# Expert stage of a fp32 transformer kernel: four consecutive rows of the down matrix per partition, its loads split by partitions

## The reference, cut to what matters

```python
def moe_swiglu(h, w_router, w_gate, w_up, w_down):
    logits = jnp.einsum('bsd,de->bse', h, w_router).astype(jnp.float32)
    top_v, top_i = lax.top_k(logits, TOP_K)          # 2 of 8 experts
    wts = jax.nn.softmax(top_v, axis=-1)
    gates = jnp.sum(jax.nn.one_hot(top_i, N_EXPERTS, dtype=jnp.float32) * wts[..., None], axis=-2)
    ...
        a = jnp.einsum('sd,edf->sef', hb, w_gate)    # w_gate, w_up: 8 x 1024 x 3584
        u = jnp.einsum('sd,edf->sef', hb, w_up)
        act = jax.nn.silu(a) * u * gb[:, :, None]
        return jnp.einsum('sef,efd->sd', act, w_down)  # w_down: 8 x 3584 x 1024
```

## Time and profile before

| | |
|---|---|
| median of 3 runs | 2482.04 us |
| lowest, highest run | 2480.72, 2488.93 us |
| span of the profiled execution | 2474.2 us |
| part of it in the stage's 56 steps | about 728 to 1708 us |

### The profile page before, as it was taken

The page is one execution under the profiler, slowest core; times in us unless marked ns, Lnnn a source line. Parts: engine busy times, 40 slices in busy tenths (PEclk is TensorE's granted clock), DMA queues, the critical chain, the costliest instruction groups (busy, mean ns, idle before and its releaser), DMA issues. The chain is left out here.

```text
span 2474.2 us, 29768 instructions
## 1 busy us (share of the span) xinstructions
PE 2244.1 (91%) x11037; PEld 1861.1 (75%) x11037; DVE 1815.4 (73%) x1813; ACT 1323.8 (54%) x1336; POOL 49.8 (2%) x130
## 2 busy tenths in 40 slices
PE   3867899797889999999999999996979998887998
PEld 3755788685668888888888888885967888766886
DVE  6987767677779988888888888886745545565444
ACT  2432434354347777777777777775444435344433
POOL 2000000000000000000000000000000000000000
PEclk9978999898899999999999999998989999988999
DMA  8852478744149999999999999997424555322553
GB/s 301 284 202 81 170 278 316 255 158 128 60 154 373 363 349 360 353 359 347 360 352 362 348 360 354 359 364 250 154 85 150 190 192 172 126 74 77 191 173 124
DMA packets 300760, 600.45 MB, mean 243 GB/s; under 512 B 20603, under 2 KB 99174, under 8 KB 300646
## 3 DMA queue, kind: packets, MB, share of 16 engines
q1 hardware_dynamic: 292928, 588.65, 67.2%
q10 hardware_dynamic: 7718, 10.19, 1.2%
HBM read 595.62 MB, written 3.15 MB: 242 GB/s over the span
## 5 line engine op out<-in xcount | busy, mean ns | idle before, releaser
L136 PE MATMUL bank<-ring_rounded,hT_rounded 128*128 128x512 f32 (+3 forms) x912 | 361.4, 396 | 17.8 <-DVE ring_rounded L297 5.7
L136 PE MATMUL bank<-ring_rounded,z_rounded 128*128 128x512 f32 x896 | 355.5, 397 | 0.2 <-DVE ats_rounded L3064 0.2
L136 PE MATMUL bank<-ring_rounded,L_rounded 128*128 128x512 f32 x712 | 283.1, 398 | 13.5 <-DVE ats_rounded L863 11.6
L3060 DVE TENSOR_TENSOR ring_rounded<-ring,zT_rounded 128x2048 fp32r<-128x2048 f32 x110 | 251.0, 2289 | 47.6 <-ACT zT_rounded L2972 47.3
L138 PE MATMUL bank<-zT_rounded,L_rounded 128*128 128x512 f32 x704 | 275.5, 391 | 0.0
L137 PE MATMUL bank<-zT_rounded,ats_rounded 128*128 128x512 f32 x704 | 275.4, 391 | 0.0
L3060 DVE TENSOR_TENSOR ring_rounded<-ring,z_rounded 128x2048 fp32r<-128x2048 f32 x111 | 251.5, 2287 | 18.5 <-ACT z_rounded L2972 17.9
L2972 ACT ACTIVATE z_rounded<-ring 128x2048 fp32r<-128x2048 f32 x111 | 210.8, 1917 | 49.0 <-DMA ring<-in_moe_w_up 31.1
L2972 ACT ACTIVATE zT_rounded<-ring 128x2048 fp32r<-128x2048 f32 x110 | 210.5, 1914 | 22.3 <-DMA ring<-in_moe_w_down 20.8
L136 PEld LDWEIGHTS bank<-ring_rounded,hT_rounded 128*128 128x128 f32 x912 | 175.9, 193 | 53.1 <-issue 14.0
L136 PEld LDWEIGHTS bank<-ring_rounded,z_rounded 128*128 128x128 f32 x896 | 168.3, 188 | 37.6 <-DVE ats_rounded L3064 1.0
(11 more groups left out here) (528 smaller groups left out, 4940.2 us busy)
## 6 DMA issues: line engine op xcount, KB each, us to landing
ring<-in_moe_w_gate SPq DMA_DIRECT2D x224, 512.0 KB, 4.7
ring<-in_moe_w_up SPq DMA_DIRECT2D x224, 512.0 KB, 5.1
ring<-in_moe_w_down SPq DMA_DIRECT2D x224, 512.0 KB, 4.5
ring<-in_ffn_w_gate_up SPq DMA_DIRECT2D x88, 512.0 KB, 5.0
ring<-in_ffn_w_down SPq DMA_DIRECT2D x66, 512.0 KB, 7.9
ring<-in_w_ada SPq DMA_DIRECT2D x48, 512.0 KB, 7.6
ring<-in_w_in SPq DMA_DIRECT2D x32, 512.0 KB, 5.1
xn<-in_w_ada SPq DMA_DIRECT2D x24, 512.0 KB, 9.6
```

Of the source, the lines that this page charges most:

```text
L136: pe.matmul(out, r32(a[0]), r32(b[1]), start=start, stop=False, skip_group_check=True)
L3060: dve.tensor_tensor(r32(w), w, high(c.hi_moe[slot]), ALU.subtract).then_inc(E[kind + '_lo'], 1)
```

## The change

The down matrix is seen as `e (s p a) n -> p (e s) (a n)`: of the 512 rows of a step, partition p holds the four consecutive rows 4p to 4p+3, 16 KB in one stretch of HBM. A slot takes the first or the second 8 KB of it. The two loads of a slot no longer take one row each of all 128 partitions. They take both rows of partitions 0 to 63, and both rows of partitions 64 to 127. Since row 4p+a now stands where row 128a+p stood, DVE writes the activation in the same order: element 4t+a of a token goes to column 128a+t, so that PE's transposes and products stay as they are.

```diff
@@ moe_load
     w, half = c.ring[:, slot, :], s % 2
     if MOE_SLOTS[s] == 'down':
-        w = w.rearrange('p (k n) -> p k n', k=2)
-        for a in range(2):
-            sp.dma_start(w[:, a:a + 1, :], c.moe_down[:, bass.ds(m * ROWS_DOWN + (2 * half + a), 1), :])\
-              .then_inc(sem, 16)
+        for q in range(2):
+            v = slice(q * HD, q * HD + HD)
+            sp.dma_start(w[v, :].unsqueeze(1), c.moe_down[v, bass.ds(m, 1), half * SLOT:half * SLOT + SLOT]).then_inc(sem, 16)
@@ moe_pass_dve, body
-        dve.tensor_tensor(c.moe_fa, c.moe_fs, c.pb[7][:, :], ALU.mult).then_inc(E['act'], 1)
+        dve.tensor_tensor(c.moe_fa.rearrange('p (a t) -> p t a', a=ROWS_DOWN), c.moe_fs.rearrange('p (t a) -> p t a', a=ROWS_DOWN),
+                          c.pb[7][:, :].rearrange('p (t a) -> p t a', a=ROWS_DOWN), ALU.mult).then_inc(E['act'], 1)
@@ build
-        c.moe_down = tensors['moe_w_down'][0].rearrange('e (k p) n -> p (e k) n', p=P)
+        c.moe_down = tensors['moe_w_down'][0].rearrange('e (s p a) n -> p (e s) (a n)', p=P, a=ROWS_DOWN)
```

## The result

The changed kernel takes 2841.88 us (median of 4 runs, 2835.97 to 2847.72), beside 2481.38 us for the kernel before: a ratio of 1.145, 95% interval 1.1423 to 1.1478. It is slower by 360 us. I had forecast 2700 us, slower, with a range up to 2775: the direction was right, and the loss is 1.65 times the 218 us I gave. The medians in this document leave out two runs in a slower state, one of halves_mirrored (2880 us) and one of the kernel before (3835 us).

The account below looks back on a forecast made before the run. PE was taken as the bound at 17.66 us a step; doubled down loads would make DMA the bound at 21.4 us, adding 215 us to a 2474.2 us span, plus 7.8, rounded to 2700 us; range 2476 to 2775.

Parts of the forecast that it names:

- The bound of before: Expert stage: PE sets the pace at 17.66 us a step, DMA second by 0.3 to 1.7 us.
- my two readings of the room: DMA's time for a step's loads: 17.4 us by the 98.3% share, or 16.0 us by the full queue's 393 GB/s.
- The split by partitions: Down loads on one half of the partitions take twice the time, 10.7 us a step instead of 5.3; chance 0.63.
- The sum, 21.4 us a step: Expert stage: 10.7 us for gate and up plus 10.7 for down, above PE's 17.66, so DMA becomes the bound.
- my 215: Expert stage: its last weight matmul ends at 1923 us instead of 1707.8, so the span grows by 215 us.
- Partial sharing as a softening: Down loads: halves overlap as engines drift; 1.8 times gives 2637 us; rival factor 1.3 to 1.8, 2490 to 2635, chance 0.10.
- Longer rows: Down loads: 8 KB rows save about 0.1 us a step, worth nothing while PE sets the pace.
- The product on DVE: L3078, 680 ns before, costs 0.1 us more, covered by 4.1 us; rival that DVE becomes late, up to +38 us, 0.03.
- The clock: Expert stage: PE 83% busy, clock might fall to 0.83, making PE's work 21.3 us; little cost inside the forecast.
- The signs: In the stage: share 100%, 294 GB/s, PE near 83%, SP's waits shrunk, down landings well above gate's, gate packets unchanged.
- The offset: Whole kernel: the median of the runs lies 7.8 us above the span, taking 2689 to 2697 us.
- my own bound by the share reading, 2797: Expert stage: from 17.4 us a step, gate and up 11.6 plus down doubled to 11.6, +315 us.

Follow-up runs that it names:

- halves_mirrored: The changed kernel with the second down slot's (slot 5's) halves loaded in the order upper, lower; 2853.83 us, ratio 1.1460.
- before_less_pe: The kernel before with one of the three matmuls of each expert-stage product left out; 2403.79 us, one run.
- every_other_partition: The changed kernel with a down slot's two loads on even and odd partitions instead of lower and upper half; 2479.12 us, ratio 0.9999.
- halves_old_view: The kernel before with only the down loads split by halves of the partitions, old row order and 4 KB packets; 2821.51 us, ratio 1.1379.
- halves_in_step: halves_old_view with SyncE waiting for all landings before the loads of each of experts 2 to 8; 2769.55 us, ratio 1.1178.
- halves_in_step_always: halves_old_view with SyncE waiting for all landings before every step's loads from the second expert on; 2807.33 us, ratio 1.1313.
- all_by_halves: The changed kernel with the gate and up loads also split by halves of the partitions; 2873.26 us, one run.
- wide_rows_all_partitions: The changed kernel with each down slot filled across all 128 partitions, one load of 7.5 KB and one of 512 B each; 2484.50 us, ratio 1.0019.

## Why the prediction was right in direction and wrong in size

**The bound of before.** Right. PE set the pace at 17.66 us a step and DMA stood 1.4 us behind it: 16.3 us by before_less_pe. Of my two readings of the room, the full queue's was the right one to take.

**The split by partitions.** Right in mechanism, and the doubling about right in size: the packet records give the changed kernel's 8 KB packets 589 ns, against 2 x 173 for the two 4 KB packets that they replace, a factor of 1.7. I wrote that the trace could not tell engine from partition; every_other_partition does. The 6% for two concurrent loads that I cited stands on the same page in another section than the one I named.

**The sum, 21.4 us a step.** This is the step that failed. I took the sum of the loads' times for the time of a step, as if all 16 engines kept a full queue and reached each load at nearly the same time. In the first steps of halves_old_view that held, 21.5 us, partly by luck: two terms were off and made up for each other. Down packets took 280 ns and not 2 x 173, and the gate and up packets, which I had left at their cost, 104 against 89 in before_less_pe. With 32 and 128 of them an engine and step and the share of 1.04 of those steps, that is 3.5 us more for down and 1.8 for gate and up, an estimate; together the 5.3 that I had put on down alone.

What broke the sum is that the engines do not stay together. In the changed kernel the last two of a slot's 32 landings come 8.7 and 10.5 us behind the first, where 30 are there after 3.3. The ring has no other slot to offer meanwhile, so the other engines run dry. Its step of 24.1 us at a share of 94.0% holds 22.7 us of packets' time, which at the share of 1.04 of those first steps would be 21.8 us, an estimate. So of the missing 2.7 us some 2.3 are engines without work and 0.4 longer packets. Over 55 steps 2.7 us are 149 us, the gap between my 215 and the measured 354 to 372. That engines out of step cost time is shown by halves_in_step, 52 us back though its waits cost SyncE 80, and by the landings; that they are nearly all of the gap rests on the sum above and on halves_in_step_always. Which engine falls behind and how it starts was not tried. My sentence that the engines reach the second load at nearly the same time was the wrong assumption behind it.

**Partial sharing as a softening.** I took drift to be a help, factor 1.8 for 2. With four of six slots on all partitions it costs. Where all loads are by halves it may help: that is my reading of 293 against 234 GB/s in all_by_halves, not a tested one.

**Longer rows.** Right at nothing: wide_rows_all_partitions and every_other_partition stand at the time of before.

**The product on DVE.** I took 0.1 us; it is 0.37 to 0.42 us. Its cover held, and the time did not move.

**The clock.** PE busy 82%, clock 0.96, better than the 0.83 I had set beside it; no cost of its own was seen, and none was tested.

**The signs.** PE's busy share and the twice as slow down packets came as I wrote. The others did not: a share of 94% for 100%, 262 GB/s for 294, gate packets at 102 ns for unchanged, a landing time of down (10.4 us) no longer than gate's (10.3). SyncE's waits for PE did not shrink, 735 of 1260 us against 534 of 920, both 58%.

**The offset.** I took the 7.8 us between span and median for time outside the span. In the four runs after it is 1.7 to 1.8 us, so most of the 7.8 was scatter between runs.

**The range.** The lower part held the wrong cases. The upper end, 2775, lay below even my own bound by the share reading, 2797, and allowed no cost beside the transfer.

## What to carry to other kernels

Split a load by rows or columns, or by alternate partitions, before you split it into the lower and upper half: the same bytes on even and odd partitions cost nothing here, with PE setting the pace, and on halves 360 us. When a stage has two limits 1.4 us apart, price the second one with a run in which the first is taken away; it tells the room better than a busy share, which read 98% with 1.4 us free, 103% with a full queue, and 94% where the loads set the pace. And once a closed ring of slots becomes the bound, add the transfers' times only as a floor: what a slot waits for is its slowest engine. Look at a slot's last landing beside the others; it shows such an engine at once.

## What the hardware showed that I had not expected

One program has two paces in one run: 293 GB/s for some 250 us and then 258 (halves_old_view), 234, 293 and 230 (all_by_halves). One of 16 engines, as I read the landings, ran 5 to 7 us behind the rest for some 1000 us, and the whole stage went at its pace. Emptying the DMA queue on purpose, seven times, made a stage that is bound by DMA 52 us faster. And DVE needs 1.05 us in place of 0.68 for 128 x 512 words when four neighbouring words are written 512 bytes apart.
